# Two- and three-term products of a transformer kernel: joined operands, latent heads in rounded parts, last down products by columns

## The reference

```python
o_mla = latent_attention(q_mla, k_mla, kv[..., MLA_NOPE:])            # 8 heads x 64
merged = (jax.nn.sigmoid(g_na + b_gate[i, :D_MODEL]) * (o_na @ w_na_o[i])
          + jax.nn.sigmoid(g_mla + b_gate[i, D_MODEL:]) * (o_mla @ w_mla_o[i]))
x = _layer_norm(DEEPNORM_ALPHA * x + merged @ w_out[i], ln1_g[i], ln1_b[i])
# first layer: f = (silu(x @ w1) * (x @ w3)) @ w2, w1 and w3 1024 x 2816, w2 2816 x 1024
# second layer: f = sum over 8 experts of gate_e * swiglu_e(x), two experts per token
x = _layer_norm(DEEPNORM_ALPHA * x + f + ple, ln2_g[i], ln2_b[i])
# hybrid layer, at the end:
return x + (jax.nn.silu(h2 @ w_gate) * (h2 @ w_up)) @ w_down          # again 1024, 2816, 1024
```

## Time and profile before

| | |
|---|---|
| median of 3 runs | 2029.85 us (2029.56 to 2030.17) |
| profiled execution | 2030.13 us |
| its span | 2028.3 us |
| TensorE busy | 1990.2 us (98%) |
| VectorE busy | 1535.9 us (76%) |
| ScalarE busy | 1012.3 us (50%) |
| DMA, mean rate over the span | 273 GB/s |
| granted TensorE clock, mean | 0.996 |

### The profile page before, as it was taken

How to read it: one execution, slowest core, us unless ns; L and a number is a source line. 1 busy time by engine, 2 the same in 40 slices (tenths; PEclk the granted TensorE clock), 3 DMA queues, 4 the chain that set the end, 5 groups by cost and what they waited for, 6 DMA issues and landing times.

```text
span 2028.3 us, 28426 instructions
## 1 busy us (share of the span) xinstructions
PE 1990.2 (98%) x11368; PEld 1714.6 (85%) x11368; DVE 1535.9 (76%) x1541; ACT 1012.3 (50%) x1064; POOL 79.9 (4%) x57
## 2 busy tenths in 40 slices
PE   8999999999999989999999999999999998999999
PEld 8988799989988778888888888888888877869998
DVE  3674677776654698888888888888888976567766
ACT  0363110011452377777777777777777753472000
POOL 0111100000001200000000000000001000100000
PEclk9999999999999999999999999999999999999999
DMA  9643588744634689999999999999999984435550
GB/s 328 197 152 110 184 297 307 270 148 129 218 125 151 235 297 384 381 379 371 385 385 375 385 381 380 370 384 385 377 384 380 408 284 151 145 105 178 196 176 33
DMA packets 184221, 553.22 MB, mean 273 GB/s; under 512 B 9296, under 2 KB 112080, under 8 KB 140864
## 3 DMA queue, kind: packets, MB, share of 16 engines
q1 hardware_dynamic: 175296, 517.55, 69.7%
q10 hardware_dynamic: 6912, 25.02, 3.0%
q0 software_dynamic: 1920, 9.34, 1.2%
HBM read 528.02 MB, written 23.59 MB: 272 GB/s over the span
## 4 chain that ended last, share of the span: by engine, by line
PE 95%; DVE 3%; ACT 2%; issue 1%; DMA 0%; DVEq 0%; ACTq 0%; SPq 0%
PE act_ps L1168 29%; PE dve_ps L1193 15%; PE act_ps L1029 15%; PE dve_ps L1029 9%; PE job_ps L1123 6%; PE dve_ps L905 6%; PE act_ps L1076 2%; PE job_ps L1056 2%; PE act_ps L905 1%; PE job_ps L1176 1%; PE job_ps L956 1%; PE job_ps L998 1%; PE job_ps L984 1%; PE act_ps L1455 1%; PE act_ps L1301 1%
## 5 line engine op out<-in xcount | busy, mean ns | idle before, releaser
L2388 DVE TENSOR_TENSOR weights_rest<-weight_ring,expert_short 128x2048 fp32r<-128x2048 f32 x336 | 763.0, 2290 | 103.1 <-ACT expert_short L1720 102.5
L1720 ACT ACTIVATE expert_short<-weight_ring 128x2048 fp32r<-128x2048 f32 x336 | 641.1, 1916 | 109.8 <-PE act_ps L1168 74.0
L1168 PE MATMUL act_ps<-expert_short,tokens_short 128*128 128x512 f32 x896 | 354.2, 395 | 4.0 <-ACT arena_o L1737 2.1
L1168 PE MATMUL act_ps<-expert_short,tokens_rest 128*128 128x512 f32 x896 | 349.2, 390 | 0.0
L1168 PE MATMUL act_ps<-weights_rest,tokens_short 128*128 128x512 f32 x896 | 349.1, 390 | 0.0
L1628 ACT ACTIVATE arena_mla<-act_ps 128x256 f32<-128x256 f32 (+1 forms) x72 | 31.0, 432 | 377.3 <-PE act_ps L1029 335.8
L1168 PEld LDWEIGHTS act_ps<-expert_short,tokens_short 128*128 128x128 f32 x896 | 168.2, 188 | 38.7 <-DVE weights_rest L2388 3.2
L1168 PEld LDWEIGHTS act_ps<-expert_short,tokens_rest 128*128 128x128 f32 x896 | 168.2, 188 | 36.2
L1168 PEld LDWEIGHTS act_ps<-weights_rest,tokens_short 128*128 128x128 f32 x896 | 168.4, 188 | 33.6
L2317 DVE TENSOR_TENSOR weights_rest<-weight_ring,ffn_weights_short 128x2048 fp32r<-128x2048 f32 x66 | 151.3, 2292 | 2.2
L1193 PE MATMUL dve_ps<-expert_short,hidden_short 128*128 128x512 f32 x448 | 139.5, 393 | 0.0
(11 more groups left out here) (408 smaller groups left out, 3721.1 us busy)
## 6 DMA issues: line engine op xcount, KB each, us to landing
weight_ring<-in_moe_w SPq DMA_DIRECT2D x336, 1024.0 KB, 7.0
weight_ring<-in_w_in SPq DMA_DIRECT2D x43, 1024.0 KB, 8.0
weight_ring<-in_ffn_w SPq DMA_DIRECT2D x32, 1024.0 KB, 7.6
weight_ring<-in_w_out SPq DMA_DIRECT2D x12, 1024.0 KB, 6.4
weight_ring<-in_w_gate SPq DMA_DIRECT2D x11, 1024.0 KB, 5.5
weight_ring<-in_w_up SPq DMA_DIRECT2D x11, 1024.0 KB, 8.0
weight_ring<-in_w_down SPq DMA_DIRECT2D x10, 1024.0 KB, 7.0
weight_ring<-in_w_ple_gate SPq DMA_DIRECT2D x8, 1024.0 KB, 6.5
```

Source lines behind the costliest of these rows:

```text
L1168: m = nc.tensor.matmul(bank[0:CAP, :], a[:, 4 * c + k, :], w[:, k, :], start=(c == k == i == 0), stop=(c == 1 and k == 3 and i == 2))
L1720: nc.scalar.activation(shorts[u % SHORTS][:, :], ring[:, slot, half], ACT.Copy).then_inc(moe_w_short, 1)
L2388: V.tensor_tensor(ring_lo[slot][:, half], ring[:, slot, half], shorts[u % SHORTS][:, :], ALU.subtract)\
```

## The change

It has three parts.

1. **Up projections.** The short and rest parts of a swiglu stage's input are addressed as one operand: `ff_x_both` is [2, 256] columns per k, 5 x 2048 words apart. `half_terms` multiplies a k tile of short weights by both at once, into the 512 columns of a bank, and the rest of the weights by the short input into the first 256. The halves of a bank are then added by a `tensor_reduce` on VectorE, over a view that takes word s and word s+256 in turn. This applies to w1 too, so that ScalarE's Silu now works from SBUF on both tiles of a pair. VectorE's weight split of a w3 unit now stands ahead of the split of the hidden values.
2. **Latent heads.** `o_mla` and its weights are split, and 8 tiles x 4 k x 3 terms replace the float32 products. ScalarE casts the two units of the weights, VectorE subtracts. VectorE's copy of the last pair's values moves behind the first two gate products.
3. **Last expert.** The products of its last down block are issued for the first 512 columns, then for the second; the put-back of the first columns stands four matmuls into the second columns, and the sums in `second_norm` follow in the order 0, 2, 1, 3.

```diff
-        ff_x = [parts("ffn_in_short", "work", [P, DT, SEQ]), parts("ffn_in_rest", "arena_o", [P, DT, SEQ])]
+        assert base_of["arena_o"] == base_of["work"] + 5 * 4 * DT * SEQ
+        ff_x_both = parts("ffn_in_both", "work", [P, 6, DT * SEQ])[:, 0:6:5, :]
+        ff_up = std[:, :, :].rearrange("p t s -> p (t s)")
+        ff_x = [tiles(ff_x_both[:, i, :], DT) for i in range(2)]
+            def half_terms(bank, w, at, k):
+
+                short, rest = w
+                both = ff_x_both[:, :, k * SEQ:(k + 1) * SEQ]
+                if k:
+                    nc.tensor.matmul(bank[:, 0:SEQ], rest[:, k, at], ff_x[0][:, k, :], start=False, stop=True, skip_group_check=True)
+                m = nc.tensor.matmul(tiles(bank[:, :], 2), short[:, k, at], both, start=k == 0, stop=True,
+                                     skip_group_check=k > 0)
+                if k == 0:
+                    nc.tensor.matmul(bank[:, 0:SEQ], rest[:, k, at], ff_x[0][:, k, :], start=False, stop=True, skip_group_check=True)
+                return m
...
                         for j in range(2):
                             at = slice(j * P, (j + 1) * P)
                             bank = act_bank() if kind == "w1" else dve_bank()
-                            m = split_product(bank[:, 0:SEQ], (short, rest), at, ff_x)
+                            for k in range(DT):
+                                m = half_terms(bank, (short, rest), at, k)
...
-                for c in range(2):
-                    down(it, GROUPS_E - 1, c)
-                pe.wait_ge(put_ready, turn + 1)
-                for b in range(4):
-                    if b < 2:
-                        pe.wait_ge(last_y[b], turn + 1)
-                    nc.tensor.matmul(acc_ps[b][:, :], put_gate[0:CAP, b // 2 * P:(b // 2 + 1) * P],
-                                     moe_y[0:CAP, b % 2 * 512:(b % 2 + 1) * 512], start=True, stop=True).then_inc(last_scattered, 1)
+
+                def put_back(columns):
+                    pe.wait_ge(last_y[columns], turn + 1)
+                    for b in PUT_ORDER[2 * columns:2 * columns + 2]:
+                        nc.tensor.matmul(acc_ps[b][:, :], put_gate[0:CAP, b // 2 * P:(b // 2 + 1) * P],
+                                         moe_y[0:CAP, columns * 512:(columns + 1) * 512], start=True, stop=True).then_inc(last_scattered, 1)
+
+                g = GROUPS_E - 1
+                pe.wait_ge(moe_h_done, it * GROUPS_E + (g + 1))
+                for columns in range(2):
+                    done = 0
+                    for c in range(2):
+                        u = moe_unit_of("w2", g, c)
+                        slot, half = unit_half(u)
+                        if columns == 0:
+                            pe.wait_ge(*rest_ready(u, it))
+                        short, rest = tiles(shorts[u % SHORTS][:, :], 2), tiles(ring_lo[slot][:, half], 2)
+                        for k in range(2):
+                            for i, (h, w) in enumerate(((h_hi, short), (h_hi, rest), (h_lo, short))):
+                                if columns == 1 and done == PUT_BEHIND:
+                                    pe.wait_ge(put_ready, turn + 1)
+                                    put_back(0)
+                                m = nc.tensor.matmul(dve_ps[columns][0:CAP, :], h[:, g % 2, 2 * c + k, :],
+                                                     w[:, k, columns * 512:(columns + 1) * 512], start=False, stop=c == k == 1 and i == 2)
+                                done += 1
+                        if columns == 1:
+                            m.then_inc(moe_unit_done, 1)
+                    if columns == 0:
+                        m.then_inc(last_columns, 1)
+                put_back(1)
...
-                heads_w.append(weights(4, D))
-                pe.wait_ge(out_copied, layer_pairs * (l + 1))
-                heads_tiles(o_mla, 0, DT)
+                heads_rest = tiles(ring_lo[n.block % RING][:, :], 4)
+                n.block += 1
+                pe.wait_ge(heads_split, l + 1)
+                for j in range(DT):
+                    bank, at = dve_bank(), slice(j * P, (j + 1) * P)
+                    for k in range(4):
+                        if j == 0 and k % 2 == 0:
+                            pe.wait_ge(heads_w_split, 2 * l + k // 2 + 1)
+                        short = tiles(in_w[k // 2][:, :], 2)[:, k % 2, at]
+                        for i, (w, o) in enumerate(((short, 0), (short, 1), (heads_rest[:, k, at], 0))):
+                            m = nc.tensor.matmul(bank[:, 0:SEQ], w, o_x[o][:, k, :], start=(k == i == 0), stop=(k == 3 and i == 2))
+                    m.then_inc(dve_tile_ready, 1)
...
+            def swiglu(units, clear=False):
+                for kind, _, _, pair, _ in units:
+                    if kind != "w1":
+                        continue
+                    n.a += 2
+                    act.wait_ge(act_tile_done, n.a)
+                    h = ff_silu[:, pair % 2, :]
+                    nc.scalar.activation(h, h, ACT.Silu).then_inc(ffn_silu_done, 1)
+                    for f in (2 * pair, 2 * pair + 1) if clear and 2 * pair < EXPERTS * PASSES else ():
...
+                heads_block = ple_block_at[l] - 3
+                act.wait_ge(*weights_landed(heads_block))
+                for c in range(2):
+                    act.wait_ge(*in_units(l)[IN_UNITS - 2 + c][2])
+                    nc.scalar.activation(in_w[c][:, :], ring[:, heads_block % RING, c * 2048:(c + 1) * 2048], ACT.Copy)\
+                        .then_inc(heads_w_short, 1)
                 nc.scalar.activation(alpha_ident, const("ident"), ACT.Copy, scale=ALPHA).then_inc(alpha_ready, 1)
...
+            def halves_of(bank):
+                return bank[:, :].rearrange("p (h s) -> p s h", h=2)
...
                 for u, (kind, _, _, pair, _) in enumerate(units):
+                    h = ff_silu[:, pair % 2, :]
                     if kind == "w1":
-                        n_act = 2
+                        if n.pair >= 2:
+                            dve.wait_ge(ffn_h_ready, n.pair - 1)
+                        for j in range(2):
+                            bank = act_ready()
+                            V.tensor_reduce(h[:, j * SEQ:(j + 1) * SEQ], halves_of(bank), AX_X, ALU.add).then_inc(act_tile_done, 1)
                     elif kind == "w3":
-                        act_tiles(n_act)
-                        h = ff_silu[:, pair % 2, :]
+                        if n.pair >= 1:
+                            dve.wait_ge(ffn_h_full, n.pair)
                         for j in range(2):
-                            part = h[:, j * SEQ:(j + 1) * SEQ]
-                            V.tensor_tensor(part, ready()[:, 0:SEQ], part, ALU.mult).then_inc(dve_tile_done, 1)
+                            bank = ready()
+                            V.tensor_reduce(ff_up[:, j * SEQ:(j + 1) * SEQ], halves_of(bank), AX_X, ALU.add).then_inc(dve_tile_done, 1)
                         dve.wait_ge(dve_tile_done, n.d)
+                        n.pair += 1
+                        dve.wait_ge(ffn_silu_done, n.pair)
+                        V.tensor_tensor(h, ff_up, h, ALU.mult).then_inc(ffn_h_full, 1)
+                    split_w(units, u + 2)
+                    if kind == "w3":
                         if pair >= 4:
                             dve.wait_ge(down_used, w_first + pair - 4)
                         short, rest = [a[:, pair % 4].rearrange("p f s -> p (f s)") for a in ff_h]
+                        dve.wait_ge(ffn_h_full, n.pair)
                         V.tensor_copy(short, h).then_inc(ffn_h_short, 1)
-                        n.pair += 1
                         dve.wait_ge(ffn_h_short, n.pair)
                         V.tensor_tensor(rest, h, short, ALU.subtract).then_inc(ffn_h_ready, 1)
-                    split_w(units, u + 2)
...
+                def heads_rest(c):
+                    block = ple_block_at[l] - 3
+                    half = slice(c * 2048, (c + 1) * 2048)
+                    dve.wait_ge(heads_w_short, 2 * l + c + 1)
+                    V.tensor_tensor(ring_lo[block % RING][:, half], ring[:, block % RING, half], in_w[c][:, :], ALU.subtract)\
+                        .then_inc(heads_w_split, 1)
                 for j in range(DT):
                     V.tensor_tensor(merged[:, j, :], ready()[:, 0:SEQ], gates[0][:, j, :], ALU.mult).then_inc(dve_tile_done, 1)
+                    if j == 1:
+                        output(layer_pairs * (l + 1) - 1)
+                        dve.wait_ge(out_copied, layer_pairs * (l + 1))
+                        V.tensor_copy(o_x[0][:, :, :], o_mla).then_inc(heads_short, 1)
+                        dve.wait_ge(heads_short, l + 1)
+                        V.tensor_tensor(o_x[1][:, :, :], o_mla, o_x[0][:, :, :], ALU.subtract).then_inc(heads_split, 1)
+                    if j in (2, 4):
+                        heads_rest(j // 2 - 1)
```

71 lines of the change are left out of this document (40 added, 31 removed).

## The result

| | before | after |
|---|---|---|
| median | 2029.89 us | 2033.16 us |
| lowest to highest of 20 runs | 2028.25 to 2031.08 | 2030.57 to 2035.03 |
| span of the profiled execution | 2028.3 us | 2031.1 us |
| TensorE busy | 1990.2 us | 1984.4 us |
| VectorE busy | 1535.9 us | 1603.6 us |

The changed kernel is slower by about 3 us: the ratio is 1.0015, with a 95% interval of 1.0009 to 1.0021. I had forecast 2017 us. The prediction also names 2033 us, as the total with slow reduces. TensorE has 5.8 us less to do, as its page line says, and the span is 2.8 us longer, so the time went into waits and into matmuls at a lower clock.

What follows compares the result with a forecast made beforehand. The prediction took TensorE's matmul issue as the bound (busy 98% of the span). Its terms, -7.9 - 5.7 + 0.6 = -13.0 us from a median of 2029.85, gave 2017 us, with 2014 to 2024 holding 8 in 10.

Steps and rivals of the forecast that it cites:

- Part 1: Up projections of both swiglu stages: 8.5 us less on TensorE, 0.6 us of stalls, sum -7.9 us.
- The price of a reduce: Up projections, VectorE adding the two halves of a bank: 0.69 us per reduce.
- the walk: VectorE followed unit by unit through the up projections: margins 0.4 and 0.23 us, no regular stall, 0.3 us a stage.
- A: Rival, up projections: the alternating reduce is slow, 1.22 us, total 2045; about 2033 at 1.04 us; chance 0.13.
- D: Rival, up projections: the longer matmul hides weight loads, the triple falls toward 335 ns, total 2011; chance 0.05.
- B: Rival, up projections: small waits between VectorE operations eat the margins, 3 to 6 us, 2020 to 2023; chance 0.18.
- C: Rival, up projections: widths in turn cost TensorE more, 10 ns per triple, 7 us, total 2024; chance 0.07.
- Part 2: Latent heads: shorter products and an earlier free bank, less a 0.46 us stall, -2.84 us per layer, -5.7 in all.
- the prediction's own sign: Latent heads: the forecast counts as wrong if one layer's heads lose less than 2 us.
- Part 3: Last expert: two put-backs delay the end of the products and the first sum, +0.6 us, bounds -1 to +1.
- the rest of the chain is as long: End of the experts: VectorE's chain of sums and statistics to the norm keeps its length after the first sum.

Runs made afterwards that it cites:

- casts_alone: The kernel before with two more ScalarE copies (3.7 us) behind the sigmoids in the first layer, into buffers nobody reads; 2031.56 us, ratio 1.0007.
- heads_alone: The kernel before with only the latent heads changed; 2035.86 us, ratio 1.0031.
- two shifted kernels: The changed kernel with idle one-word memsets early in VectorE's program, moving its later code by 196 or 68 instructions; 2031.44 us (ratio 1.0003) and 2030.15 us (0.9999).
- last_alone: The kernel before with only the last expert changed; 2031.47 us, ratio 1.0007.

## Why the prediction was wrong

**Part 1 was right.** The stages are 3.8 and 3.7 us shorter, forecast 3.95. The price of a reduce and the walk came out: in the rows of 1945 to 1952 the next split is usable 5.0 us and both w1 tiles are reduced 7.2 us after the w3 unit's end, where I had 5.16 and 7.30. Rivals A and D fall with it. B, small waits in the margins, didn't show: TensorE's one wait in the two stages is 0.2 us, ahead of the first up product of the second. Of C, put at 10 ns a triple, 2 ns are there (349.4 in place of 347.6).

**Part 2 failed at the overlap that it called hidden.** The step read: ScalarE's casts come 3.7 us later, GpSimd's two subtractions "then end near 194, needed at about 204: hidden". They ended at 195.7, early enough for that need; the question was wrong. I asked who needs the result, and not whom the work meets on its way. An addition of VectorE with two operands in SBUF stood still while GpSimd's subtraction ran, 3.8 us for an instruction of 0.42, and casts_alone shows it in the kernel before. That the two would meet was to be read beforehand: the earlier trace rows end at 190.2, and the first addition came at 191.7. The Trainium skill has the rule (SBUF — State Buffer, section SBUF: two separate sides: a VectorE instruction with two SBUF inputs and a GpSimd instruction that reads SBUF exclude each other for a whole instruction); the rows here agree with it, 4.22 and 2.56 us for the additions and 10.22 for GpSimd's pair, and I had not weighed it. The term was -2.8 per layer; found were +2.5 and +3.5, so the prediction's own sign, less than 2 us won in one layer's heads, was met in both. Without GpSimd in the way the step is -2.6 us, 0.2 short.

The clock made it dearer. I had priced a stall of TensorE at its own length. Behind the wait of 3.4 us the clock was 0.5 to 0.6 in three of the four layers of the changed kernel and heads_alone, which cost 1.4 to 2.4 us more; the fourth had none of it. The two shifted kernels have the same heads, and all four of their layers show the low clock; none of the ten kernels without this wait does, in the same stretches. What makes the one exception is open.

**Part 3 was right in its own terms**, 0.6 us, shown by last_alone, but a term outside it failed: "the rest of the chain is as long". It held a jump whose price depends on where the code lies, and part 1 moved the code. The branch was there to be seen, between copy and sum in the kernel before, and I took it for free because it was. This is 2.8 us. TensorE, idle for 7 us, then starts the transposes at 0.56 of its clock (windows of the changed kernel):

```profile
1682.00:1684.00 2.00, 0.00 (x0) 0.00 (x0) 1.93 (x6) 0.89 (x4) 1.13 (x2) 0.50 0.09 30
1684.00:1688.00 4.00, 4.00 (x18) 3.64 (x19) 2.88 (x7) 1.01 (x4) 0.07 (x1) 0.56 0.90 298
```

That isn't a second loss of the same kind: the kernel before, idle for 3.8 us there, has 0.57 at the same transposes (1679 to 1683 us).

**What is left.** The 0.7 us at the start, the -1.2 us behind the first stage and the +1.2 us between the sums and the second stage have no cause in the change that a run has shown. For the last two the clock tells where they lie. At 454 to 457 us it is 0.50 in the kernel before, and 1.00 in this stretch of the changed one; at 1800 to 1803 us it is 0.53 in the changed kernel, and 1.00 in the same stretch before. Such a dip ahead of the second stage stands in five of the fourteen kernels traced, with and without each part of the change. The medians of the groups of runs of the kernel before differ by less than 1 us, its single runs by over 5.

The sum: -7.5 (part 1), +6.0 (heads), +0.6 (part 3), +2.8 (jump), +0.9 (the rest) is +2.8 us, the difference of the spans. No rival of the prediction was what happened. Its 0.07 for slower rested on A alone. The chances show the fault of method: 0.18 for small waits on an engine that I had walked unit by unit, and nothing for a collision with one that I had called hidden.

## What to carry to other kernels

An engine that is called hidden has to be checked twice: when its result is needed, and which instructions of other engines it runs beside. In these traces GpSimd reading SBUF and VectorE with two SBUF operands shut each other out for whole instructions (4.22 us for 0.42). Where that holds, keep long GpSimd instructions away from short VectorE ones on the critical path, or give the work to VectorE.

A branch, even one over code that is never run, can have a price that depends on the number of instructions ahead of it, here 0 or 2.8 us. If a stretch behind a branch moves by 2 to 3 us and the edit was elsewhere, shift the code by some dozens of idle instructions before explaining it.

When parts of a change are to be judged, one run of each part tells more than the sum: here +6, -5 and +1.5 us (the last within the noise) stood behind a result of +3.
